# A two-layer hybrid decoder on one core: adaptive-norm sums moved out of the projections, and the compression layer with swapped operands

## The reference, cut to what matters

```python
u = x * (1 + scale1) + shift1
x = LayerNorm(alpha * x + (1 + gate1) * Mixer(u))
u = x * (1 + scale2) + shift2
x = LayerNorm(alpha * x + (1 + gate2) * SwiGLU(u))
```

```python
flat = blk.transpose(0, 1, 3, 2, 4).reshape(B, nc, G, CMP_BLOCK * Dh)
return jax.nn.gelu(flat @ w1) @ w2
```

## Time and profile before

| | |
|---|---|
| median of 3 runs | 1960.57 us |
| the profiled execution, first to last instruction | 1955.2 us |
| busy: TensorE, its weight loads | 91%, 73% |
| busy: VectorE, ScalarE, GpSimd | 52%, 32%, 19% |
| mean granted clock of TensorE | 0.949 of full |

### The profile page before, as it was taken

One profiled execution on the slowest core, in us unless ns is written; L12 is line 12 of the kernel. 1 busy time (PEld: TensorE's weight loads), 2 busy tenths in 40 slices (PEclk: granted clock), 3 DMA queues, 4 the chain that ended last, 5 costly groups with the idle time before them and its releaser, 6 DMA issues.

```text
span 1955.2 us, 21770 instructions
## 1 busy us (share of the span) xinstructions
PE 1770.7 (91%) x8565; PEld 1427.8 (73%) x8565; DVE 1013.1 (52%) x1375; ACT 625.2 (32%) x1122; POOL 380.0 (19%) x274
## 2 busy tenths in 40 slices
PE   5789889999997999999967789899999899999997
PEld 5568766767775888888846677667777678888885
DVE  4973845555656434333377585555556643333334
ACT  1320234444525222222152022444443342222223
POOL 2653650000004514000055565000000020000000
PEclk8886999999998999999988689999999999999999
DMA  8444531001232534333324545110112223333331
GB/s 312 131 143 145 164 108 34 22 23 43 84 96 84 171 114 142 97 89 99 103 76 140 172 130 165 40 33 22 33 55 86 86 75 92 101 92 100 90 98 54
DMA packets 285972, 192.90 MB, mean 99 GB/s; under 512 B 8072, under 2 KB 272816, under 8 KB 284848
## 3 DMA queue, kind: packets, MB, share of 16 engines
q1 hardware_dynamic: 271920, 148.79, 25.9%
q0 software_dynamic: 12032, 42.07, 6.9%
q10 hardware_dynamic: 1920, 0.66, 0.1%
HBM read 189.39 MB, written 2.10 MB: 98 GB/s over the span
## 4 chain that ended last, share of the span: by engine, by line
PE 73%; DVE 15%; ACT 5%; DMA 4%; issue 3%; SPq 0%; DVEq 0%; ACTq 0%
PE banks L1365 20%; PE banks L1367 20%; PE banks L1366 20%; PE banks L1430 3%; DVE w_lo L856 3%; PE banks L1463 2%; PE banks L1488 2%; ACT probs L764 2%; PE banks L1549 2%; DVE t L935 1%; DVE kdT L939 1%; DMA ring<-in_cmp_w_k_dram 1%; DMA ring<-in_w_in_dram 1%; PE banks L1432 1%; DMA ada_first_a<-in_w_ada_dram 1%
## 5 line engine op out<-in xcount | busy, mean ns | idle before, releaser
L1365 PE MATMUL banks<-u_hi,w_hi 128*128 128x512 f32 x1328 | 550.7, 415 | 69.6 <-DVE w_lo L856 36.9
L1366 PE MATMUL banks<-u_lo,w_hi 128*128 128x512 f32 x1328 | 528.3, 398 | 0.0
L1367 PE MATMUL banks<-u_hi,w_lo 128*128 128x512 f32 x1328 | 528.0, 398 | 0.0
L856 DVE TENSOR_TENSOR w_lo<-ring,w_hi 128x1024 fp32r<-128x1024 f32 (+1 forms) x246 | 329.9, 1341 | 359.1 <-ACT w_hi L613 357.9
L613 ACT ACTIVATE w_hi<-ring 128x1024 fp32r<-128x1024 f32 (+1 forms) x246 | 255.2, 1039 | 345.7 <-PE banks L1367 234.0
L1365 PEld LDWEIGHTS banks<-u_hi,w_hi 128*128 128x128 f32 x1328 | 257.3, 194 | 124.2 <-DVE w_lo L856 40.8
L1367 PEld LDWEIGHTS banks<-u_hi,w_lo 128*128 128x128 f32 x1328 | 255.5, 192 | 55.9
L1366 PEld LDWEIGHTS banks<-u_lo,w_hi 128*128 128x128 f32 x1328 | 257.2, 194 | 44.9
L555 POOL TENSOR_SCALAR res<-yT,mul_r,add_r 128x512 f32<-128x512 f32 x24 | 32.2, 1347 | 913.5 <-DVE yT L978 913.5
L544 POOL TENSOR_TENSOR ada_acc<-ada_acc,ada_ring 128x1024 f32<-128x1024 f32 x70 | 192.7, 2753 | 6.2
L1367 PE MATMUL banks<-h_hi,w_lo 128*128 128x512 f32 x352 | 136.9, 389 | 0.0
(11 more groups left out here) (211 smaller groups left out, 2216.4 us busy)
## 6 DMA issues: line engine op xcount, KB each, us to landing
ring<-in_w_ffn_in_dram SPq DMA_DIRECT2D x88, 512.0 KB, 3.7
ada_ring<-in_w_ada_dram POOLq DMA_DIRECT2D x80, 512.0 KB, 4.1
ring<-in_w_in_dram SPq DMA_DIRECT2D x78, 512.0 KB, 3.6
ring<-in_w_ffn_out_dram SPq DMA_DIRECT2D x32, 448.0 KB, 3.6
ring<-in_w_out_dram SPq DMA_DIRECT2D x16, 512.0 KB, 3.7
ring<-in_w_ffn_out_dram SPq DMA_DIRECT2D x16, 512.0 KB, 3.7
ada_first_a<-in_w_ada_dram SPq DMA_DIRECT2D x5, 1024.0 KB, 9.1
ring<-in_cmp_w_k_dram SPq DMA_DIRECT2D x8, 512.0 KB, 4.6
```

Of the source, the lines that this page charges most:

```text
L856: V.tensor_tensor(lo, src, hi.bitcast(fp32), ALU.subtract).then_inc(split_lo, 1)
L1365: M(bank, wh[:, block], sh[:, k, :], start=start, stop=False)
L1366: M(bank, wh[:, block], sl[:, k, :], start=False, stop=False)
L1367: return M(bank, wl[:, block], sh[:, k, :], start=False, stop=stop)
```

## The change

The groups get other places. In layer 0, groups 2 to 5 are summed before gm4, gm6, gm8 and gm10, within attention, and GpSimd begins them after the first scores of layer 0. All six groups of layer 1 are made beside the feed-forward part of layer 0, before fa5, fa8, fa11, fa14, fa17 and fa20. No group is left in any projection, and none in layer 1. gate1 gets one copy for each layer.

In the compression layer flat (128 rows, 64 columns) becomes the stationary operand and w1 (256 columns) the moving one; k goes to output partitions 0 to 63 and v to 64 to 127, in turn, 32 products in all. w1 no longer passes through the ring: it is loaded into a place of its own (which attention uses later) in eight pieces of 512 KB, one ahead of each of the ring loads vs to kd0. gelu is applied once, two transposes (`turn_hidden`, behind kd0) bring the hidden part into the old layout, and the products with w2 come behind kd1 (`compressed`). VectorE saves both behind the rotations of kd0 and kd1. The unused columns of flat are set to zero.

```diff
-          + ["hk", "hv", "kv2"] + [f"kd{i}" for i in range(4)] + [f"qd{i}" for i in range(4)]
+          + ["hid", "kd0", "hidT", "kd1", "kv2", "kd2", "kd3"] + [f"qd{i}" for i in range(4)]
...
-ADA_BEFORE = {"qn1": 2, "kd1": 3, "vd1": 4, f"gm{GM_IN}": 5, "fa10": 0, "fa20": 1}
+FIRST_ADA = {"gm4": 2, "gm6": 3, "gm8": 4, "gm10": 5}
+NEXT_ADA = {"fa5": 0, "fa8": 1, "fa11": 2, "fa14": 3, "fa17": 4, "fa20": 5}
 
 
 def ada_before(l, name):
 
-    j = ADA_BEFORE.get(name)
-    if j is None or (j < 2 and l + 1 == DEPTH):
-        return None
-    return (l + 1 if j < 2 else l, j)
+    if l == 0 and name in FIRST_ADA:
+        return (0, FIRST_ADA[name])
+    if l + 1 < DEPTH and name in NEXT_ADA:
+        return (l + 1, NEXT_ADA[name])
+    return None
 
...
-        + ["kd0", "kd1"] + [f"w1{a}{i}" for a in "kv" for i in range(4)]
-        + [f"{a}{i}" for a in ("kd", "qd", "vd") for i in range(4)][2:]
...
-SPLIT = [name for name in JOBS if name[:2] != "w1"]
+SPLIT = JOBS
+W1_WITH = ["vs", "vw", "g", "qn0", "qn1", "qn2", "qn3", "kd0"]
+W1_ROWS = CMP_BLOCK * HEAD_DIM // 4
...
+        w1_all = at("w1", 20, 16)
...
+            def load_w1(l, n):
+
+                if n == 0 and l == 0:
+                    sp.wait_ge(x_turned, KD)
+                    sp.wait_ge(vec_turned, DEPTH)
+                    sp.wait_ge(setup_done, 1)
+                    sp.wait_ge(lam_summed, 1)
+                    wait_done(sp, 0, "ada01")
+                elif n == 0:
+                    wait_done(sp, l - 1, f"fo{KD - 1}")
+                w, part = n % 2, n // 2
+                src = (w1_k, w1_v)[w][l, W1_ROWS * part:W1_ROWS * (part + 1), :]
+                sp.dma_start(w1[:, w, 4 * part:4 * part + 4, :], src.rearrange("(j p) n -> p j n", p=P))\
+                    .then_inc(w1_in, 16)
 
...
-                elif name[:2] == "w1":
-                    m, half = divmod(int(name[-1]), 2)
-                    w1 = w1_k if name[2] == "k" else w1_v
-                    srcs = [cols(w1[l, KD * P * half:KD * P * (half + 1), :], P * m, P * (m + 1))]
...
+                    if name in W1_WITH:
+                        load_w1(l, W1_WITH.index(name))
                     load(l, name)
...
             pool.wait_ge(part1, 1)
+            pool.wait_ge(scored, 1)
             ada_groups(0, 4)
             for l in range(DEPTH):
                 residual(l, 0)
                 if l + 1 < DEPTH:
-                    ada_groups(4 + 6 * l, 6 + 6 * l)
+                    ada_groups(4 + 6 * l, 10 + 6 * l)
                     residual(l, 1)
-                    ada_groups(6 + 6 * l, 10 + 6 * l)
 
 
...
-                for w, name in enumerate(("hk", "hv")):
-                    wait_done(act, l, name)
-                    dst = hid[:, w].rearrange("p m (g n) -> p m g n", g=2)[:, :, :, 0:NC]
-                    src = bank_of(l, name)[:, 0:128].rearrange("p (m g n) -> p m g n", m=2, g=2)[:, :, :, 0:NC]
-                    nc.scalar.activation(dst, src, ACT.Gelu_apprx_tanh).then_inc(saved(l, name), 1)
+                wait_done(act, l, "hid")
+                nc.scalar.activation(hid_tok, bank_of(l, "hid")[:, 0:CMP_HIDDEN], ACT.Gelu_apprx_tanh)\
+                    .then_inc(saved(l, "hid"), 1)
...
+                    V.memset(flat[:, w].rearrange("p j (g n) -> p j g n", g=2)[:, :, :, NC:NCP], 0.0)
...
+                def save_hidden():
+
+                    wait_done(dve, l, "hidT")
+                    src = bank_of(l, "hidT")[:, 0:2 * P].rearrange("p (m w n) -> p m w n", m=2, w=2)
+                    V.tensor_copy(hid[:, :, :], src[:, :, 0, :])
...
+                            hid_rep[:, m],
+                            src[:, m, 1, :].rearrange("p (g n) -> p g n", g=2).unsqueeze(2)
+                            .to_broadcast([P, 2, 4, NCP]))
+                    last.then_inc(saved(l, "hidT"), 1)
...
+                        if a == "kd" and i == 0:
+                            save_hidden()
+                        elif a == "kd" and i == 1:
+                            save_compressed()
...
+            def hidden(l):
+
+                bank = take_bank(l, "hid")
+                pe.wait_ge(flat_ready, 2 * l + 2)
+                pe.wait_ge(w1_in, 16 * len(W1_WITH) * (l + 1))
+                for j in range(KJ):
+                    for w in range(2):
+                        last = M(bank[64 * w:64 * w + 64, 0:CMP_HIDDEN], flat[:, w, j, :], w1[:, w, j, :],
+                                 start=j == 0, stop=j == KJ - 1)
+                done(l, "hid", last)
+
+            def turn_hidden(l):
+
+                bank = take_bank(l, "hidT")
+                wait_saved(pe, l, "hid")
+                for m in range(2):
+                    last = nc.tensor.transpose(bank[:, m * P:(m + 1) * P], hid_tok[:, m * P:(m + 1) * P], ident)
+                done(l, "hidT", last)
+
+            def compressed(l):
+
+                bank = take_bank(l, "kv2")
+                wait_saved(pe, l, "hidT")
+                for m in range(2):
+                    M(bank[:, 0:2 * NCP], w2k[:, l, m].rearrange("p a d -> p (a d)"), hid[:, m, :],
+                      start=m == 0, stop=m == 1)
+                for g in range(2):
+                    for m in range(2):
+                        last = M(bank[:, 64 + 64 * g:128 + 64 * g],
+                                 hid_rep[:, m, g].rearrange("p r n -> p (r n)"), w2v[:, l, m, :],
+                                 start=m == 0, stop=m == 1)
+                done(l, "kv2", last)
...
                 name = f"gm{m}"
                 if k == 0:
+                    sum_ada(l, name)
...
                 for i in range(4):
-                    sum_ada(l, f"qn{i}")
                     project(l, f"qn{i}")
                     if i == 0:
                         turn_tokens(l, "g")
-                for w, name in enumerate(("hk", "hv")):
-                    bank = take_bank(l, name)
-                    pe.wait_ge(flat_ready, 2 * l + 2)
-                    for m in range(2):
-                        dst = bank[:, 2 * NCP * m:2 * NCP * (m + 1)].rearrange("p (g n) -> p g n", g=2)[:, :, 0:NC]
-                        for j in range(KJ):
-                            if j % KD == 0:
-                                slot = weights_in(pe, l, f"w1{name[1]}{2 * m + j // KD}")
-                            last = M(dst, slot[:, (j % KD) * P:(j % KD + 1) * P],
-                                     flat[:, w, j, :].rearrange("p (g n) -> p g n", g=2)[:, :, 0:NC],
-                                     start=j == 0, stop=j == KJ - 1)
-                            if j % KD == KD - 1 and (m, j) != (1, KJ - 1):
-                                last.then_inc(w1_read, 1)
-                    done(l, name, last)
-                bank = take_bank(l, "kv2")
-                wait_saved(pe, l, "hk")
-                for m in range(2):
-                    M(bank[:, 0:2 * NCP], w2k[:, l, m].rearrange("p a d -> p (a d)"), hid[:, 0, m, :],
-                      start=m == 0, stop=m == 1)
-                pe.wait_ge(rep_ready, l + 1)
-                for g in range(2):
-                    for m in range(2):
-                        last = M(bank[:, 64 + 64 * g:128 + 64 * g],
-                                 hid_rep[:, m, g].rearrange("p r n -> p (r n)"), w2v[:, l, m, :],
-                                 start=m == 0, stop=m == 1)
-                done(l, "kv2", last)
+                hidden(l)
                 for name in [f"{a}{i}" for a in ("kd", "qd") for i in range(4)]:
-                    sum_ada(l, name)
                     project(l, name)
+                    if name == "kd0":
+                        turn_hidden(l)
+                    elif name == "kd1":
+                        compressed(l)
                 for i in range(4):
-                    sum_ada(l, f"vd{i}")
                     project(l, f"vd{i}")
                     if i:
...
```

More of the change, by code:

```diff
@@ L90 @@
 JOBS = (["kc", "vc", "ksl", "kwn", "vs", "vw", "g"] + [f"qn{i}" for i in range(4)]
-        + ["kd0", "kd1"] + [f"w1{a}{i}" for a in "kv" for i in range(4)]
-        + [f"{a}{i}" for a in ("kd", "qd", "vd") for i in range(4)][2:]
+        + [f"{a}{i}" for a in ("kd", "qd", "vd") for i in range(4)]
         + [f"gm{i}" for i in range(16)] + [f"br{i}" for i in range(KD)] + [f"wo{i}" for i in range(KD)]
@@ L354, in build @@
         part_read = sem("part_read")
-        w1_read = sem("w1_read")
+        w1_in = sem("w1_in")
         token_saved = sem("token_saved")
@@ L439, in wait_read @@
             def wait_read(l, name):
[L441 to L446, removed]
+                sp.wait_ge(split_lo, split_job(l, name) + 1)
+            def load_w1(l, n):
[11 more added lines that the diff above has]
+                    .then_inc(w1_in, 16)
             def load(l, name):
@@ L911, in save_ada @@
                 elif j in (2, 5):
-                    V.tensor_scalar(gate1[:, j // 3, :], ada[:, l, 8 * j:8 * j + 8], 1.0, None, ALU.add)
```

(34 more changed lines are left out.)

13 lines of the change are left out of this document (4 added, 9 removed).

## The result

The changed kernel takes 1882.8 us (median of 4 runs, 1879.8 to 1887.8) against 1961.3 for the kernel before in the same session: a ratio of 0.960, 95% interval 0.9585 to 0.9619. The forecast was 1880. The profiled execution, the fastest of the four, spans 1878.0 us, 77.2 less than before.

The account below looks back on a forecast made before the run. VectorE, held by GpSimd, was taken to bound the projections, with the compression layer a second hole. Gains 60 + 67.4 + 1.8 less attention's 21 and the FFN's 27.5 make 80.7: 1880 us, range 1862 to 1898.

Parts of the forecast that it names:

- 126.4 + 11: Projections, kc's save to attention, either layer: 126.4 us built up from single instructions, plus 11 for the swapped compression layer.
- H: Time of the swapped compression layer's 32 products: taken as 11 us, between 6.9 (halves at once) and 13.8 (in series).
- Layer 0's 8 us of set-up: Layer 0 before the projections: without GpSimd's first group beside it, kc's save moves 8 us, from 68.4 to 60.2.
- Rival 1: Projections of both layers: the loads are late next, 7.2 us a chunk for eight chunks, 28 more, 1908 us; chance 0.10.
- sign of being wrong: Projections: ScalarE's w_hi waiting for ring loads was listed among what would show the forecast wrong.
- 3.7 for each: Layer 0's FFN: TensorE waits 3.7 us for GpSimd's group at each of five places, 18.7 in all.
- 36.4 with its 0.35 of signalling: Layer 0's FFN: GpSimd's time per group, between 35.0 and 38.3 plus 0.35, against 32.6 us of TensorE between places.
- 2 (c): Layer 0's attention: held VectorE instructions with two SBUF inputs cost 0 to 54 us; 14, a quarter, taken.
- The wait before gm6: Layer 0's attention: TensorE waits 2 us there for a GpSimd group, the places gm4 and gm6 being 31.3 us apart.
- the clock's row: Profile row where a TensorE wait of 3.12 us was followed by products at clock 0.50; priced in the FFN, once 1.6 us.
- a sign that the prediction had named: Layer 0's attention longer than layer 1's by over 40 us would show the forecast wrong.
- The 5.4 us around the span: Whole kernel: 5.4 us added to the profiled span of 1955.2 to make the median of 1960.57, and likewise to 1874.5.

Follow-up runs that it names:

- experiment 4: Changed kernel with the compression products of k all before those of v, instead of in turn; 1896.5 us, ratio 0.967.
- Experiment 7: Changed kernel without GpSimd's multiplications and additions, but for one per group, in layer 1's six groups beside layer 0's FFN; 1868.0 us.
- experiment 3: Changed kernel without GpSimd's multiplications and additions, but for one per group, in layer 0's four groups in attention; 1852.8 us.
- experiment 5: Changed kernel with each GpSimd multiplication and addition cut in four of 256 columns; 1954.7 us, ratio 0.997.

## Why the prediction was right

**The bound.** The reading that VectorE, held by GpSimd, bounds the projections was right: w_lo 1.22 and rotations without a long product, clock 1.00, 132.1 us from kc's save to attention in both layers. Built up from single instructions I had 126.4 + 11. H was sized from products split by rows, 11.2; it measured 7.13, the low end, and experiment 4 shows why. The Trainium skill (TensorEngine Tiling (Array Packing), Key Properties) says that tiles multiply in parallel; by that rule H is an estimated 6.9, and this trace agrees with 7.13. The other 126.4 measured 125. Layer 0's 8 us of set-up were right (kc's save at 60.2). Rival 1's sign of being wrong did turn up: ScalarE's w_hi waited for ring loads six times in layer 0's projections, 16.9 us in all, the longest 4.2. But TensorE waited for w_lo there only 1.2 us in all, and the clock stayed at 1.00. So the ring covered the waits, as forecast, and nothing is left for rival 1.

**The FFN.** Mechanism and places were right: the steps to fa8, fa11, fa14 and fa17 are 3 to 4 us longer than with a sum alone and that to fa20 1 us. The forecast had 3.7 for each. Groups took 34.4 to 35.2 us there, where the forecast had 36.4 with its 0.35 of signalling; 21.2 lost instead of 27.5. Experiment 7 confirms the cause. TensorE stands idle only a part of these 3 us: 2.0 us before fa8, 1.2 before the next three, 0.8 before fa20. The rest is work at the low clock, as here behind the sum before fa11:

```profile
719.77 1.92 PE L1368 MATMUL banks<-cst,ada_acc 128*128 128x1 f32 x16 [1.17 <-POOLq L559]
```

```profile
724.00:726.00 2.00, 2.00 (x6) 1.51 (x6) 0.07 (x1) 0.00 (x0) 1.41 (x2) 0.50 0.66 174
```

It costs nothing more, since GpSimd's next group sets when the next sum can start; the forecast had said so.

**Attention.** Here the size was off by two: 43.7 us were lost where 21 were forecast. The failed step is 2 (c): "From 0 to 54, I take 14, a quarter". Of the 45.6 us, 7.6 are the four sums; 38 are what was to be 14 and 2. The wait before gm6 didn't come: attention had stretched so far that GpSimd was done 11 us early. VectorE's held time was even less than I had counted: it was busy 28.6 us longer, of which experiment 3 takes 26 away, and not 54. Few instructions were held, 5 of the 16 tiny scalars and 1 of the 16 mixes among them. The set I had counted was not complete either: two saves of the vectors with one SBUF input (128x8) took 2.13 and 0.90 us instead of 0.17. What I had left out is what a held instruction does to TensorE here. One case of the changed kernel, VectorE, then GpSimd beside it, then TensorE:

```profile
227.19 1.31 DVE L1138 SCALAR_TENSOR_TENSOR d_mix<-d_mix,sums,neg_lam 128x1 f32<-128x1 f32 x1
228.54 2.52 DVE L1140 SCALAR_TENSOR_TENSOR probs<-probs,d_mix 128x128 f32<-128x128 f32 x1
```

```profile
227.36 1.13 POOL L556 TENSOR_SCALAR ada_ring<-ada_ring,c_silu 128x1024 f32<-128x1024 f32 x1
...
228.58 2.33 POOL L557 TENSOR_TENSOR ada_acc<-ada_acc,ada_ring 128x1024 f32<-128x1024 f32 x1
```

```profile
228.08 0.40 PE L1389 MATMUL banks<-u_hi,w_lo 128*128 128x512 f32 x1
231.20 0.45 PE L1518 MATMUL banks<-cst,probs 128*128 128x128 f32 x1 [2.73 <-DVE probs L1140]
...
234.17 0.63 PE L1388 MATMUL banks<-u_lo,w_hi 128*128 128x512 f32 x1
```

and the windows of the same stretch:

```profile
228.00:230.00 2.00, 0.47 (x3) 0.03 (x1) 1.96 (x2) 0.39 (x1) 1.91 (x2) 1.00 0.85 256
230.00:232.00 2.00, 0.80 (x5) 0.83 (x5) 2.00 (x3) 0.31 (x2) 1.41 (x2) 0.79 0.02 6
232.00:234.00 2.00, 1.70 (x9) 1.29 (x10) 1.89 (x6) 0.66 (x4) 0.08 (x1) 0.50 0.50 88
```

A scalar that takes 0.22 us alone takes 1.31 and ends with GpSimd's multiplication, at 228.5. The mix behind it takes 2.52 instead of 0.35 and ends with the add, at 231. TensorE is idle 2.73 us and then works at half the clock. I had applied the clock's row to the FFN alone. Over the stage this shows as TensorE's 22 us of busy time, of which the four sums are 7.6 and the slow clock the other 14; experiment 3, without GpSimd's arithmetic, gets 11 of the 14 back. The 24 us of idle time are about the 26 that VectorE was held, and experiment 3 gets 23 of them back. By this balance nearly all of the held time was on the chain, not a quarter of it, and it drew nearly half its length again in slow clock. I did not follow the held instructions one by one. It was also a sign that the prediction had named: layer 0's attention is 46 us longer than layer 1's, where over 40 was to mean wrong. With 38 in place of 16 the forecast would have been 1902, outside the range. That the forecast of 1880 lies 3 us from the result is luck: H and the rest of the projections in both layers gave 11 us more than forecast, the FFN 6 and what is left 2, together 19 of the 23 that attention cost more.

**The 5.4 us around the span.** These were misread, without harm. In every run listed the time is 1.8 to 2.1 us above the span, as in 1879.8 against 1878.0; so the other 3.6 or so were that the profiled execution of the kernel before was faster than its median.

**The clock.** In the case above TensorE is busy 0.47 and 0.80 us of two stretches of 2 us, and the granted clock then stands at 0.50, the 1.2 GHz level, from 232 us on. The Trainium skill (TensorE: Matmul & The Clock Gate, What's actually happening) describes these two levels, the lower one as the state after idleness; the trace agrees.

## What to carry to other kernels

Ask of each VectorE instruction with two SBUF inputs whether it is on the chain before putting GpSimd work beside it: here tiny ones were held as long as large ones (0.22 us became up to 2.10, w_lo's 1.21 up to 2.79). Work that has to lie beside such a chain should come in short instructions, with the places of its results far enough apart for the longer total. Where TensorE consumes groups from one accumulator, the distance of the places must exceed the time of a group, first of all for the first group; and a wait of TensorE is to be priced with the slow clock behind it, unless, as in the FFN here, something else sets the pace of the next stretch anyway.

## What the runs showed of the hardware that I had not expected

Two f32 products with 128 rows, 64 stationary columns each and output partitions 0 to 63 and 64 to 127, in turn, take 0.111 us per 256-column instruction; in blocks of one half 0.207.

A GpSimd instruction has a part that doesn't shrink with its width. Multiplications of 128x256 take 0.46 us at the shortest and 0.54 in the mean (experiment 5), where 128x1024 takes 1.11 and 1.18 (changed kernel); additions 0.71 and 0.82, where 128x1024 takes 2.33 and 2.55. Four quarters of an addition take 20 to 30% longer, four of a multiplication 70 to 80%. From the shortest ones I estimate the fixed part at 0.2 us.
